# A decoder's cross attention and expert router read unnormalised rows; the norm's root is applied later

## The chip, the cores and the metric

One core of a Trainium2 chip runs the whole program. The metric is the device time of one execution in microseconds (us). The change is judged against the kernel before on the same chip.

## The reference, cut to what matters

Three layers run on 512 tokens of width 1024 in float32. The first two are hybrid layers (feed-forward, selective attention, RWKV-7, gated delta rule), which the change doesn't touch. The third mixes, attends to 256 memory rows, and sends each token to 2 of 16 experts:

```
h = h + hybrid_mixer(rms_norm_2(h, mix_norm[l]), ...)
h = h + memory_cross_attention(rms_norm_2(h, cross_norm[l]), mem_n, w_xq[l], w_xk[l], w_xv[l], w_xo[l])
h = h + hierarchical_moe(rms_norm_2(h, moe_norm[l]), w_router_group[l], ...)

rms_norm_2(x, gain): x * rsqrt(mean(x*x, -1) + EPS) * gain
memory_cross_attention: q = h @ w_xq (4 heads of 128);  s = q k^T * 128**-0.5;  softmax(s) v;  @ w_xo
hierarchical_moe:
    g_prob = softmax(h @ w_rg + b_rg)                 # 4 groups
    grp = argmax(g_prob); p_grp = g_prob[grp]
    e_logits = (h @ w_re + b_re)[group grp]           # 4 experts of that group
    top_p, top_i = top_k(softmax(e_logits), 2)
    gate = p_grp * top_p / sum(top_p)
    # rows of h are sorted by expert into blocks of 128 (23 blocks), each block goes through its expert,
    # and the results come back weighted by gate
```

The root `rsqrt(mean(x*x))` is one number per token. A product of an unnormalised row with a weight matrix can therefore be multiplied by it afterwards.

## The kernel before, in words

Each engine has its own program, written out by hand in order; engines meet through counted semaphores (`act.step(name)` raises one, `e.wait_ge(*act.at(name))` waits for it). The residual stream `xT` lies with channels on partitions, as 8 chunks of 128 x 512 tokens. Weights come through a ring of two 1 MB slots (`ring`), issued by SyncE in the order of `sources`; a slot's load waits until the slot's last holder has let go of it. After the ring's end SyncE streams the experts' weights in 1 MB pieces, six deep, four of them in `arena`.

Two kinds of product occur. **Split products**: ScalarE copies the weights to `w_hi` (rounded, `split_act`, L340), VectorE writes the remainder `w_lo` (`split_dve`, L344), the rows are split likewise into `x_hi` (L429 or L657) and `x_lo` (L434 or L661), and TensorE makes three passes of 128x512 for each product (hi*hi, lo*hi, hi*lo; L456, L469, L513, L652). **Whole products** take float32 operands as they are; TensorE shows two records for each.

A **norm** (`norm_pe`, `norm_act`, `norm_dve`): ScalarE squares the 8 chunks as the residual of each is done (L365), GpSimd adds seven of them (L372), TensorE sums over channels (`mean_pe`, L379), ScalarE takes the root (L384), VectorE the reciprocal (L389), TensorE spreads it over partitions (L394), and VectorE writes the normalised chunks `xn` (L420). In feed-forward layers the kernel before already works otherwise: `rows_act_in` makes `x_hi` (times the gain, without the root) and the square of each chunk right after its residual, `gate_first_pe` (L456) multiplies chunk by chunk, and the root is applied to the result.

Around the change the work stands in this order:

- `out_pe` of "mix2_out": four split slots, the last products at L513, each chunk's residual added by VectorE (L527).
- `cross_pe`, `cross_act`, `cross_dve`: the norm; queries for four heads by whole products (heads 0 and 1 chunk by chunk at L734, heads 2 and 3 at L718); ScalarE copies them out (L2716); both engines split the two slots of `w_xo` (XO_AT); then two strands of softmax attention (`attention_pe`, `attention_act`, `attention_dve`) run woven, 8 blocks each: scores (L1867), maximum (L1907), its negative times the scale (L1915), exponential (L1935), scaling (L1901), transposes (L1876), copy (L1946), values (L1885), copy (L1952).
- `out_pe` of "cross_out": two split slots (L652, L513), residuals.
- `router_pe`, `router_act`, `router_dve`: the norm; logits by whole products, 128x20 each (L734); 32 transposes that turn the rows to token order (L2748, copied out at L2770); VectorE splits the first three expert pieces (L2929), adds the bias (L2781), makes two softmaxes over groups and experts (`softmax4`, with exponentials on ScalarE at L2768 and L2773) with the choice of group and of two experts (up to `chosen`, L2840); TensorE ranks the tokens of each expert (L2752 to L2757); VectorE turns ranks into row numbers (`rows`, L2878).
- `experts_pool`: GpSimd scatters the token rows by eight indirect DMAs (L3080). SyncE loads the first two blocks of rows back, and the experts start (L2954, L3002, L3009, L2943).

Of the kernel before, what the change touches and what calls it, by code (L numbers as in the profile page):

```python
# [164 lines left out]
def build(nc, x_in, mem_in, const_in, w1_in, w2_in, y_out):  # L165
    with ExitStack() as ctx:
# [103 lines left out]
        for at, n, who in ((0, 17, pe), (17, 4, dve), (21, 2, pe), (23, 2, dve), (25, 1, pe)):  # L270
            slots(two_at + at, n, who)
# [280 lines left out]
        norm_order["cross"] = norm_order["moe"] = from_bank(0)  # L552

# [1298 lines left out]
        class Block:  # L1852
            def __init__(self, width, products, mask, values, part, dst):
                self.width, self.products, self.mask = width, products, mask
                self.values, self.part, self.dst = values, part, dst

# [33 lines left out]
        def attention_dve(e, M, blocks, first, scale):  # L1890
            tag, n = M.tag, len(blocks)
            for i in range(n + 2):
# [9 lines left out]
                if i < n:  # L1902
# [12 lines left out]
                    e.tensor_scalar(nm, mx, -scale, None, ALU.mult).then_inc(*dve.step(("nm", tag, g)))  # L1915
# [3 lines left out]
        def attention_act(e, M, blocks, first, scale):  # L1919
            tag, n = M.tag, len(blocks)  # L1920
            for i in range(n + 2):
# [5 lines left out]
                if i < n:  # L1927
# [4 lines left out]
                    if b.mask is None:  # L1932
                        if g >= 2:
                            e.wait_ge(*pe.at("turn", tag, g - 2))
                        e.activation(p_row, M.SCORES[:, :b.width], ACT.Exp, bias=nm, scale=scale, accum_out=sm).then_inc(  # L1935
                            *act.step(("exp", tag, g), ("read", tag, g)))
# [745 lines left out]
        def cross_room(F):  # L2682
            X, A = Room(), Arena(4 * SLOT)
            X.k_, X.v = F.k_mem, F.v_mem
            X.q_ = A.take(4 * SEQ).rearrange("p (c t) -> p c t", c=4)
            X.attend = [softmax_room(("cross", n), A, banks, at) for n, banks, at in (
# [3 lines left out]
        def cross_blocks(X, n):  # L2690
            blocks = []
            for q in range(NT):
                for h in (n, n + 2):
                    blocks.append(Block(
                        MEM, [(X.q_[:, h, q * P:(q + 1) * P], X.k_[:, h, :])], None,
                        lambda s, h=h: X.v[:, s, h * P:(h + 1) * P], slice(0, P), mixed[:, h, q * P:(q + 1) * P]))
            return blocks

        def cross_pe(e, X):
            norm_pe(e, "cross")  # L2700
            w = columns(XQ_AT)
            e.wait_ge(*there(XQ_AT))
            by_chunk(e, "cross", lambda c, n: (w[:, c, n * P:(n + 1) * P], xn[:, c, :]),
                     [bank[n][:, :] for n in range(2)]).then_inc(
                *pe.step(("cross_q", 0), ("cross_q", 1), ("slot", XQ_AT)))
            e.wait_ge(*there(XQ_AT + 1))
            for c in range(2):
                by_channel(e, XQ_AT + 1, c * P, bank[2 + c][:, :], xn).then_inc(
                    *pe.step(("cross_q", 2 + c), *([("slot", XQ_AT + 1)] if c else [])))
# [780 lines left out]
```

## Time and profile before

| what | before |
|---|---|
| median of 3 runs | 3636.42 us (3635.45 to 3636.93) |
| span of the profiled execution | 3662.9 us |
| TensorE busy | 3480.6 us, 95% |
| VectorE, ScalarE, GpSimd busy | 53%, 38%, 12% |
| mean granted TensorE clock | 0.949 of full |

The span is that of one execution under the profiler, from the first to the last instruction; it is the only time the profile gives of that execution, and it is 26.5 us (0.7%) above the median of the timed runs. In the rows below a time is us from the span's start; "busy" of TensorE counts matmuls whose ends are modelled; PEclk is the granted clock as a share of full speed, 1.00 or 0.50 for the two levels. What stands in brackets at a row's end is the idle time of that engine before it and what ended it.

### The profile page before, as it was taken

To read this page: it belongs to the slowest core of one execution; us is meant where nothing else is said; L and a number is where in the kernel's file an instruction comes from. 1 tells how busy PE (TensorE), PEld (TensorE's weight loads), DVE (VectorE), ACT (ScalarE), POOL (GpSimd) and SP (SyncE) were. 2 spreads that over 40 slices of the span, in tenths; PEclk is the share of its full clock that TensorE was granted. 3 is DMA by queue.
4 is the path that set the end of the run, shared out by engine and by line. 5 is a ranking of instruction groups with operands and counts; after the bars stand their busy time and mean duration, and the time that the engine had idled before them with its cause. 6 is when DMAs were issued, how large, how long until landed. Compare 5 with 4: busy or idle time off the path is not lost. (4 is left out here: it accounts for less than half of the span.)

```text
span 3662.9 us, 43142 instructions
## 1 busy us (share of the span) xinstructions
PE 3480.6 (95%) x17900; PEld 2807.1 (77%) x17900; DVE 1925.6 (53%) x2891; ACT 1383.2 (38%) x1924; POOL 431.8 (12%) x217
## 2 busy tenths in 40 slices
PE   8999998999999999999999999999999998699995
PEld 6888797876888888887878767888787675588884
DVE  4434457774453445343567754434344333489885
ACT  3222345533321232123455433222244333377772
POOL 1000342000100010002420001000131000122222
PEclk9999999986999999999989989999999999699997
DMA  4443220001223222222200002222220210599993
GB/s 173 148 144 109 81 81 1 1 24 47 81 92 111 92 93 92 104 92 81 92 13 1 1 24 107 100 94 92 109 88 27 78 58 35 224 372 408 408 408 142
DMA packets 65986, 414.61 MB, mean 113 GB/s; under 512 B 6912, under 2 KB 11136, under 8 KB 22272
## 3 DMA queue, kind: packets, MB, share of 16 engines
q1 hardware_dynamic: 63488, 403.46, 29.5%
q0 software_dynamic: 2304, 8.39, 0.6%
q8 instruction: 142, 2.33, 0.3%
q14 instruction: 52, 0.43, 0.0%
HBM read 375.13 MB, written 36.70 MB: 112 GB/s over the span
## 5 line engine op out<-in xcount | busy, mean ns | idle before, releaser
L344 DVE TENSOR_TENSOR w_lo<-ring,w_hi 128x2048 fp32r<-128x2048 f32 x146 | 334.5, 2291 | 869.6 <-ACT w_hi L340 869.6
L340 ACT ACTIVATE w_hi<-ring 128x2048 fp32r<-128x2048 f32 x146 | 280.3, 1920 | 1001.0 <-PE bank L469 584.5
L469 PE MATMUL bank<-x_hi,w_lo 128*128 128x512 f32 x1344 | 533.5, 397 | 0.0
L469 PE MATMUL bank<-x_hi,w_hi 128*128 128x512 f32 x1344 | 527.3, 392 | 0.0
L469 PE MATMUL bank<-x_lo,w_hi 128*128 128x512 f32 x1344 | 524.2, 390 | 0.0
L469 PEld LDWEIGHTS bank<-x_lo,w_hi 128*128 128x128 f32 x1344 | 252.3, 188 | 62.1
L469 PEld LDWEIGHTS bank<-x_hi,w_lo 128*128 128x128 f32 x1344 | 252.3, 188 | 58.0
L469 PEld LDWEIGHTS bank<-x_hi,w_hi 128*128 128x128 f32 x1344 | 252.3, 188 | 54.4
L513 PE MATMUL bank<-h_hi,w_hi 128*128 128x512 f32 x704 | 274.0, 389 | 0.0
L513 PE MATMUL bank<-h_hi,w_lo 128*128 128x512 f32 x704 | 274.0, 389 | 0.0
L513 PE MATMUL bank<-h_lo,w_hi 128*128 128x512 f32 x704 | 273.8, 389 | 0.0
L372 POOL TENSOR_TENSOR tmp<-tmp 128x512 f32<-128x512 f32 x54 | 76.1, 1409 | 1091.5 <-ACT tmp L365 1085.1
L2924 ACT ACTIVATE e_hi<-arena 128x2048 fp32r<-128x2048 f32 x92 | 176.3, 1916 | 23.9 <-PE bank L2943 21.1
L2929 DVE TENSOR_TENSOR e_lo<-ring,e_hi 128x2048 fp32r<-128x2048 f32 x45 | 150.1, 3335 | 44.3 <-ACT e_hi L2924 44.3
L2929 DVE TENSOR_TENSOR e_lo<-arena,e_hi 128x2048 fp32r<-128x2048 f32 x70 | 157.9, 2283 | 6.0 <-ACT e_hi L2924 6.0
L513 PEld LDWEIGHTS bank<-h_lo,w_hi 128*128 128x128 f32 x704 | 132.2, 188 | 27.6
L513 PEld LDWEIGHTS bank<-h_hi,w_lo 128*128 128x128 f32 x704 | 132.1, 188 | 27.5
L513 PEld LDWEIGHTS bank<-h_hi,w_hi 128*128 128x128 f32 x704 | 132.2, 188 | 27.4
L2934 POOL TENSOR_TENSOR e_lo<-arena,e_hi 128x2048 fp32r<-128x2048 f32 x22 | 102.0, 4634 | 318.3 <-ACT e_hi L2924 318.3
L703 PE MATMUL bank<-x_hi,ring_r 128*128 128x512 f32 x352 | 139.1, 395 | 0.0
L998 POOL TENSOR_TENSOR ring_r<-ring,first 128x1024 fp32r<-128x1024 f32 x6 | 14.4, 2421 | 1045.0 <-ACT first L990 1045.0
L998 POOL TENSOR_TENSOR ring_r<-ring,high 128x1024 fp32r<-128x1024 f32 x44 | 110.8, 2543 | 194.3 <-ACT high L990 194.3
(565 smaller groups left out, 6965.0 us busy)
## 6 DMA issues: line engine op xcount, KB each, us to landing
ring<-slots SPq DMA_DIRECT2D x238, 1024.0 KB, 4.8
arena<-slots SPq DMA_DIRECT2D x92, 1024.0 KB, 8.2
x_rows<-v_first SPq DMA_DIRECT2D x23, 512.0 KB, 6.8
xn<-x_rows SPq DMA_DIRECT2D x23, 512.0 KB, 7.9
y_rows<-xn SPq DMA_DIRECT2D x23, 512.0 KB, 8.5
x_aside<-xT SPq DMA_DIRECT2D x3, 2048.0 KB, 6.3
xT<-x_aside SPq DMA_DIRECT2D x3, 2048.0 KB, 7.9
xT<-x_t SPq DMA_DIRECT2D x2, 1024.0 KB, 10.4
```

Source lines behind the costliest of these rows:

```text
L340: e.activation(w_hi[:, k % 2, :], ring[:, k % RING, :], ACT.Copy).then_inc(*act.step(("hi", k)))
L344: e.tensor_tensor(w_lo[:, k % 2, :], ring[:, k % RING, :], w_hi[:, k % 2, :].bitcast(F32), ALU.subtract).then_inc(*dve.step(("slot", k)))
L372: e.tensor_tensor(SUM[:, :], SUM[:, :], squares[i][:, :], ALU.add).then_inc(*pool.step(("sum", tag, i)))
L469: made = e.matmul(bank[b + f][:, :], w.rearrange("p (k n) -> p k n", k=KC)[:, c, f * P:(f + 1) * P], (x_hi, x_lo)[part][:, c, :], start=c ...
L513: made = e.matmul(bank[d][:, :], w.rearrange("p (f n) -> p f n", f=2)[:, f, d * P:(d + 1) * P], rows[part][:, 2 * n + f, :], start=n == 0 ...
L703: made = e.matmul(out, w[:, c0:c0 + P], x, start=i == 0 and m == 0, stop=i == KC - 1 and m == 2)
L998: e.tensor_tensor(half_slot(ring_r[:, k % RING, :], half), raw, half_slot(high_of(N, n), half).bitcast(F32), ALU.subtract).then_inc(*pool. ...
L2924: e.activation(e_hi[m % W_BUFS][:, :], e_ring[m % E_RING], ACT.Copy).then_inc(*act.step(("expert_hi", m)))
L2929: e.tensor_tensor(e_lo[m % W_BUFS][:, :], e_ring[m % E_RING], e_hi[m % W_BUFS][:, :].bitcast(F32), ALU.subtract).then_inc(*dve.step(("expe ...
L2934: e.tensor_tensor(e_lo[m % W_BUFS][:, :], e_ring[m % E_RING], e_hi[m % W_BUFS][:, :].bitcast(F32), ALU.subtract).then_inc(*pool.step(("exp ...
```

## The change: what it does

- **Cross queries.** The rows are made as in the feed-forward layers: `rows_act_in` writes `x_hi` and squares, the residual loop of "mix2_out" writes `x_lo`, and `gate_first_pe` and `gate_up_pe` make the queries as split products of 2 x 48 passes. The two query slots (XQ_AT) are therefore split by ScalarE and VectorE. The root is applied per token inside the softmax: the exponential takes the column `X.plus` (root * 128**-0.5) as its scale, and the negated maximum is multiplied by `X.minus`. TensorE no longer spreads the root and VectorE no longer writes `xn`.
- **w_xo.** Slot XO_AT is split between the copies of queries 1 and 2. Slot XO_AT + 1 is split by a third strand of the weave, `later`, which lets eight turns of the attention pass first.
- **Router.** ScalarE writes `moe_rows` (chunk times gain, no root) into `xn` as the residuals come; the logits of all four token tiles go to one bank, chunk by chunk; the mean is taken before the last chunk. VectorE multiplies the 128x80 logits by the root and adds the bias in two instructions. The copies of the transposed rows take the root as their scale, and come before the splits of the expert pieces on ScalarE.
- **Choice and gates.** The choice is made on the logits; both softmaxes are gone from before `chosen`. Exponentials and gates are made once, after the row numbers: ScalarE's single exponential (128x20) stands after the expert splits, VectorE's three expert splits and five gate instructions after `slots`.

The diff, cut to its core:

```diff
@@ slots
-        for at, n, who in ((0, 17, pe), (17, 4, dve), (21, 2, pe), (23, 2, dve), (25, 1, pe)):
+        for at, n, who in ((0, 17, pe), (17, 4, dve), (21, 2, dve), (23, 2, dve), (25, 1, pe)):
...
@@ attention_dve, attention_act
-                    e.tensor_scalar(nm, mx, -scale, None, ALU.mult).then_inc(*dve.step(("nm", tag, g)))
+                    e.tensor_scalar(nm, mx, -scale if b.minus is None else b.minus, None, ALU.mult).then_inc(
+                        *dve.step(("nm", tag, g)))
...
+                        e.activation(p_row, M.SCORES[:, :b.width], ACT.Exp, bias=nm, scale=scale if b.scale is None else b.scale,
+                                     accum_out=sm).then_inc(*act.step(("exp", tag, g), ("read", tag, g)))
...
@@ cross
         def cross_pe(e, X):
-            norm_pe(e, "cross")
-            w = columns(XQ_AT)
-            e.wait_ge(*there(XQ_AT))
-            by_chunk(e, "cross", lambda c, n: (w[:, c, n * P:(n + 1) * P], xn[:, c, :]),
-                     [bank[n][:, :] for n in range(2)]).then_inc(
-                *pe.step(("cross_q", 0), ("cross_q", 1), ("slot", XQ_AT)))
...
+            gate_first_pe(e, "cross", XQ_AT, 0)
+            gate_up_pe(e, XQ_AT + 1, 2, None)
...
+        def later(split, e, k):
+            for _ in range(8):
+                yield
+            split(e, k)
+
         def cross_act(e, X):
-            norm_act(e, "cross", [dve.at("res", "mix2_out", 0, c) for c in range(KC)])
+            rows_act_in(e, "cross", par2("cross_norm"), [
+                [dve.at("res", "mix2_out", 0, c)] + ([pe.at("down", ("mix2_out", 0), 7)] if c >= 6 else [])
+                for c in range(KC)])
+            split_act(e, XQ_AT + 1)
+            root_act(e, "cross", side_of("cross"))
             for n in range(4):
-                e.wait_ge(*pe.at("cross_q", n))
+                e.wait_ge(*pe.at("used", XQ_AT + n // 2))
                 e.activation(X.q_[:, n, :], bank[n][:, :], ACT.Copy).then_inc(*act.step(("cross_q", n)))
-            for n in range(2):
-                split_act(e, XO_AT + n)
-            weave(*((1, attention_act(e, X.attend[n], cross_blocks(X, n), 0, P ** -0.5)) for n in range(2)))
+                if n == 1:
+                    split_act(e, XO_AT)
+            weave(*((1, attention_act(e, X.attend[n], cross_blocks(X, n), 0, P ** -0.5)) for n in range(2)),
+                  (1, later(split_act, e, XO_AT + 1)))
...
@@ router
         def router_pe(e):
...
+            for i, c in enumerate(norm_order["moe"]):
+                e.wait_ge(*act.at("moe_row", c))
+                if i == KC - 1:
+                    mean_pe(e, "moe", bank[7])
+                for t in range(NT):
+                    made = e.matmul(bank[0][:, 20 * t:20 * t + 20], moe_rows[c][:, t * P:(t + 1) * P], w[:, c, 0:20],
+                                    start=i == 0 and t == 0, stop=i == KC - 1 and t == NT - 1)
...
         def router_act(e):
...
+                e.activation(moe_rows[c], xT[:, c, :], ACT.Copy, scale=par2("moe_norm")[:, c:c + 1]).then_inc(
+                    *act.step(("moe_row", c)))
+                square_act(e, "moe", i, None)
+            root_act(e, "moe", bank[7])
...
         def router_dve(e):
-            norm_dve(e, "moe", par2("moe_norm"))
-            for n in range(LOOK):
-                split_expert_dve(e, n)
+            root_dve(e, "moe")
...
-            softmax4("groups", ex, logits[:, :, 0:4])
...
-            softmax4("experts", es, es)
...
+            for n in range(LOOK):
+                split_expert_dve(e, n)
+            second = col[:, 112:116]
+            e.wait_ge(*act.at("gates"))
+            e.tensor_reduce(mx, ex, AX, ALU.add).then_inc(*dve.step())
...
@@ scalar_program, vector_program
-            out_act(e, "mix2_out", OUT_AT[2], 4, None, {4: [dve.at("gla_out", NT - 1)]}, 2, 4)
+            out_act(e, "mix2_out", OUT_AT[2], 4, XQ_AT, {4: [dve.at("gla_out", NT - 1)]}, 2, 4)
```

The first place where the order matters is ScalarE from the queries into the attention. `w_hi` is a weight split, `tmp<-xT` a square, `arena<-bank 128x512` a copy of one head's queries, `arena,col<-bank,col` an exponential. Before:

```order
L340 ACTIVATE w_hi<-ring 128x2048 x2
L365 ACTIVATE tmp<-xT 128x512 x8
L384 ACTIVATE col<-bank,eps 128x4
L2716 ACTIVATE arena<-bank 128x512 x4
L340 ACTIVATE w_hi<-ring 128x2048 x2
L1935 ACT_TABLE_LOAD
L1935 ACTIVATE arena,col<-bank,col 128x256 x4
```

With the change, up to the split that stands inside the attention:

```order
L340 ACTIVATE w_hi<-ring 128x2048
L384 ACTIVATE col<-bank,eps 128x4
L2719 ACTIVATE arena<-bank 128x512 x2
L340 ACTIVATE w_hi<-ring 128x2048
L2719 ACTIVATE arena<-bank 128x512 x2
L1938 ACT_TABLE_LOAD
L1938 ACTIVATE arena,col<-bank,col 128x256 x4
L1949 ACTIVATE arena<-bank 128x256 x2
L1938 ACTIVATE arena,col<-bank,col 128x256 x2
L1949 ACTIVATE arena<-bank 128x256 x2
L1955 ACTIVATE mixed<-bank 128x128 x2
L340 ACTIVATE w_hi<-ring 128x2048
```

One of the two splits of `w_xo` has moved in front of the last two query copies, the other behind the third step of the attention; VectorE's `w_lo` of that slot stands between its third and fourth step likewise.

The second place is VectorE in the router, from the residuals to the choice of the group (`e_lo` is the remainder of an expert piece, `xn` a normalised chunk). Before:

```order
L527 SCALAR_TENSOR_TENSOR xT<-bank,xT 128x512 x8
L389 RECIPROCAL col<-col 128x4
L420 SCALAR_TENSOR_TENSOR xn<-xT,par,bank 128x512 x8
L2929 TENSOR_TENSOR e_lo_65<-arena,e_hi_61 128x2048
L2929 TENSOR_TENSOR e_lo_66<-arena,e_hi_62 128x2048
L2929 TENSOR_TENSOR e_lo_67<-arena,e_hi_63 128x2048
L2781 TENSOR_TENSOR col<-bank,par 128x20 x4
```

With the change, the same start, and the end behind the row numbers:

```order
L527 SCALAR_TENSOR_TENSOR xT<-bank,xT 128x512 x8
L389 RECIPROCAL col<-col 128x4
L2810 TENSOR_TENSOR col<-bank,col 128x80
L2813 TENSOR_TENSOR col<-col,par 128x80
L2834 TENSOR_REDUCE col<-col 128x4
...
L2902 CAST ids<-col 128x7
L2952 TENSOR_TENSOR e_lo_65<-arena,e_hi_61 128x2048
L2952 TENSOR_TENSOR e_lo_66<-arena,e_hi_62 128x2048
L2952 TENSOR_TENSOR e_lo_67<-arena,e_hi_63 128x2048
L2907 TENSOR_REDUCE col<-col 128x4
```

The eight normalised chunks are gone and the three splits stand behind the last cast of `ids`, where GpSimd scatters.

The third is TensorE in the router. Before:

```order
L513 MATMUL bank<-x_hi,w_lo 128x512
L379 MATMUL bank<-const,tmp 128x1 x8
L394 MATMUL bank<-const,col 128x128 x4
L734 MATMUL bank<-ring,xn 128x20 x32
L2748 MATMUL bank<-const,xn 128x128 x32
```

With the change:

```order
L513 MATMUL bank<-x_hi,w_lo 128x512
L2763 MATMUL bank<-ring,xn 128x20 x28
L379 MATMUL bank<-const,tmp 128x1 x8
L2763 MATMUL bank<-ring,xn 128x20 x4
L2772 MATMUL bank<-const,xn 128x128 x32
```

The logits stand directly behind the last output product, with the mean between the seventh and the eighth chunk.

## Rows read from the trace of the kernel before

**Rows 1.** Timeline of TensorE, end of mix2_out to the attention: start, us, instruction.

```profile
3024.04 0.39 PE L513 MATMUL bank<-x_hi,w_lo 128*128 128x512 f32 x1
3031.58 15.69 PE L734 MATMUL bank<-xn,ring 128*128 128x512 f32 x32 [0.93 <-DVE xn L420]
3047.11 13.90 PE L718 MATMUL bank<-xn,ring 128*128 128x512 f32 x32
3071.16 2.08 PE L1867 MATMUL bank<-arena 128*128 128x256 f32 x4 [8.33 <-ACT arena L1935]
3077.43 1.03 PE L1867 MATMUL bank<-arena 128*128 128x256 f32 x4
```

**Rows 2.** Timeline of ScalarE at the attention's start.

```profile
3061.05 0.60 ACT L2716 ACTIVATE arena<-bank 128x512 f32<-128x512 f32 x1 [6.27 <-PE bank L718]
3067.68 1.28 ACT L1935 ACT_TABLE_LOAD   x1
3070.54 0.47 ACT L1935 ACTIVATE arena<-bank,col 128x256 f32<-128x256 f32 x1 [1.58 <-DVE col L1915]
```

**Rows 3.** Timeline of TensorE in the router.

```profile
3119.59 0.39 PE L513 MATMUL bank<-x_hi,w_lo 128*128 128x512 f32 x1
3121.61 1.95 PE L379 MATMUL bank<-const,tmp 128*128 128x1 f32 x16 [1.64 <-POOL tmp L372]
3127.13 13.82 PE L734 MATMUL bank<-ring,xn 128*128 128x20 f32 x64 [0.93 <-DVE xn L420]
3140.78 5.39 PE L2748 MATMUL bank<-const,xn 128*128 128x128 f32 x32
```

**Rows 4.** Windows of the router: us, busy of PE, PEld, DVE, ACT, POOL, then PEclk, DMA, GB/s.

```profile
3120.00:3124.00 4.00, 1.95 (x16) 1.86 (x16) 0.80 (x2) 2.18 (x3) 1.42 (x2) 0.97 0.50 170
3136.00:3139.00 3.00, 3.00 (x16) 3.00 (x15) 2.20 (x1) 0.00 (x0) 0.00 (x0) 0.50 0.00 0
3153.00:3157.00 4.00, 3.60 (x16) 3.49 (x16) 0.77 (x7) 0.00 (x0) 0.00 (x0) 0.50 0.01 2
```

**Rows 5.** Timeline of VectorE in the router: ranks come back, row numbers are done.

```profile
3156.78 0.17 DVE L2850 TENSOR_SCALAR col<-bank 128x16 f32<-128x16 f32 x1 [3.13 <-PE bank L2757]
3159.87 0.17 DVE L2878 CAST ids<-col 128x8 int32<-128x8 f32 x1
```

**Rows 6.** GpSimd's first scatter, then TensorE's first turn of the experts' rows.

```profile
3160.90 1.17 POOL L3080 DMA_INDIRECT x_rows<-mixed,ids  x1 [39.34 <-issue]
3178.02 1.97 PE L2954 MATMUL bank<-const,xn 128*128 128x128 f32 x8 [21.28 <-DMA xn<-x_rows]
```

**Rows 7.** Layer 1's feed-forward start: TensorE, ScalarE, VectorE.

```profile
2257.57 0.39 PE L456 MATMUL bank<-x_hi,w_hi 128*128 128x512 f32 x1
2270.45 1.05 PE L394 MATMUL bank<-const,col 128*128 128x128 f32 x8
2252.76 0.71 ACT L429 ACTIVATE x_hi<-xT,par 128x512 fp32r<-128x512 f32 x1
2261.74 2.88 DVE L434 SCALAR_TENSOR_TENSOR x_lo<-xT,par,x_hi 128x512 fp32r<-128x512 f32 x2
```

**Rows 8.** Attention, third and fourth step: ScalarE, then VectorE.

```profile
3077.75 0.46 ACT L1952 ACTIVATE mixed<-bank 128x128 f32<-128x128 f32 x2
3078.71 0.47 ACT L1935 ACTIVATE arena<-bank,col 128x256 f32<-128x256 f32 x1 [0.50 <-DVE col L1915]
3076.64 0.15 DVE L1898 RECIPROCAL col<-col 128x1 f32<-128x1 f32 x1
3078.06 0.42 DVE L1907 TENSOR_REDUCE col<-bank 128x1 f32<-128x256 f32 x1 [0.88 <-PE bank L1867]
```

**Rows 9.** The page, splits on ScalarE and VectorE: busy, mean ns of one, idle before.

```profile
L340 ACT ACTIVATE w_hi<-ring 128x2048 fp32r<-128x2048 f32 x146 | 280.3, 1920 | 1001.0 <-PE bank L469 584.5
L2929 DVE TENSOR_TENSOR e_lo<-ring,e_hi 128x2048 fp32r<-128x2048 f32 x45 | 150.1, 3335 | 44.3 <-ACT e_hi L2924 44.3
L2929 DVE TENSOR_TENSOR e_lo<-arena,e_hi 128x2048 fp32r<-128x2048 f32 x70 | 157.9, 2283 | 6.0 <-ACT e_hi L2924 6.0
```

More of the change, by code:

```diff
@@ L2697, in cross_blocks @@
+                    blocks.append(b)
             return blocks
         def cross_pe(e, X):
-            norm_pe(e, "cross")
-            w = columns(XQ_AT)
-            e.wait_ge(*there(XQ_AT))
-            by_chunk(e, "cross", lambda c, n: (w[:, c, n * P:(n + 1) * P], xn[:, c, :]),
-                     [bank[n][:, :] for n in range(2)]).then_inc(
-                *pe.step(("cross_q", 0), ("cross_q", 1), ("slot", XQ_AT)))
[L2706 to L2709, printed above, removed]
+            gate_first_pe(e, "cross", XQ_AT, 0)
@@ L2721, in cross_dve @@
         def cross_dve(e, X):
-            norm_dve(e, "cross", par2("cross_norm"))
-            for n in range(2):
-                split_dve(e, XO_AT + n)
-            weave(*((1, attention_dve(e, X.attend[n], cross_blocks(X, n), 0, P ** -0.5)) for n in range(2)))
+            split_dve(e, XQ_AT + 1)
+            root_dve(e, "cross")
+            own(e, dve)
+            e.tensor_scalar(X.plus, rstd_col, P ** -0.5, None, ALU.mult).then_inc(*dve.step())
+            e.tensor_scalar(X.minus, rstd_col, -P ** -0.5, None, ALU.mult).then_inc(*dve.step())
@@ L2730, in build @@
+            split_dve(e, XO_AT)
+            weave(*((1, attention_dve(e, X.attend[n], cross_blocks(X, n), 0, P ** -0.5)) for n in range(2)),
+                  (1, later(split_dve, e, XO_AT + 1)))
         ids_row, ids_slot = ids[:, 0:8], ids[:, 8:15]
@@ new lines, in router_pe @@
+            made.then_inc(*pe.step(("logits",), ("slot", k)))
+            for t in range(NT):
+                for half in range(2):
+                    b, before = turned_bank(t, half), 2 * t + half - len(turned_banks)
+                    if before >= 0:
+                        e.wait_ge(*act.at("token_rows", before // 2, before % 2))
+                    for n in range(4):
+                        made = e.transpose(b[:, n * P:(n + 1) * P], moe_rows[4 * half + n][:, t * P:(t + 1) * P], ident)
+                    made.then_inc(*pe.step(("token_rows", t, half)))
@@ new lines, in router_act @@
+            root_act(e, "moe", bank[7])
+            for t in range(NT):
+                for half in range(2):
+                    e.wait_ge(*pe.at("token_rows", t, half))
+                    if t == 0 and half == 0:
+                        e.wait_ge(*dve.at("rstd", "moe"))
+                    e.activation(token_rows[:, t, 512 * half:512 * half + 512], turned_bank(t, half)[:, :], ACT.Copy,
+                                 scale=rstd_col[:, t:t + 1]).then_inc(*act.step(("token_rows", t, half)))
@@ L2779, in router_dve @@
             e.wait_ge(*pe.at("logits"))
[L2780 to L2783 removed]
+            own(e, dve)
+            e.tensor_tensor(logits, bank[0][:, 0:80].rearrange("p (t n) -> p t n", t=NT), wide(rstd_col, [P, NT, 20]),
+                            ALU.mult).then_inc(*dve.step())
```

103 lines of the change are left out of this document (43 added, 60 removed).

## The prediction

> **What bounds the kernel now.** I read the page first: TensorE is busy 95% of the span, so a change pays only where TensorE stands idle, runs at its lower clock, or does work that another form does faster. Then I took the timelines of TensorE, ScalarE and VectorE between the end of the mixer's output product and the first expert, about 157 us, because all that the change moves lies there; the instruction orders of the two kernels are the same up to the splits that feed this stretch.
>
> In the cross stage the last output product starts at 3024.04 and the next could start 0.23 us later, at 3024.27. The first query product starts at 3031.58, after the norm, and the queries take 15.69 and 13.90 us, until 3061.01 [rows 1]. The last copy of a query starts 0.04 us later, but the first exponential only at 3070.54: VectorE has to write both remainders of w_xo first, and the second slot is loaded late, since its ring slot is held until the queries are done [rows 2]. So 46.3 us pass between the output product and the first exponential.
>
> In the router the last product ends at 3119.82. The norm comes, then 64 records of 128x20 logits from 3127.13 to 3140.95, at 0.216 us each; the 32 transposes take 5.39 us [rows 3]. The granted clock is 0.97 over 3120 to 3124, then 0.50, and it stays there all through the logits. It is 0.50 again for the ranking products, whose 16 records are busy 3.60 us [rows 4]. VectorE receives the ranks at 3156.78 and has the row numbers at 3160.04 [rows 5]. The scatter starts 0.86 us later and TensorE turns the first rows at 3178.02 [rows 6]. From the row numbers on, nothing that TensorE waits for changes its length, so the expert stage and the end move as one block by what is gained ahead.
>
> **The change: cross stage.** Layer 1's feed-forward start is the same code and gives the measure. There 36 passes, the mean and 12 passes fill TensorE from 2257.57 to 2270.45, 12.9 us, without a gap [rows 7]. I copy that: 3024.27 + 12.9 = 3037.2. The second slot is 48 passes. The 36 passes before the mean there took 8.3 us, 0.231 each, so 11.1 us more: 3048.3, and its result is seen 0.16 us later. The added ScalarE work, x_hi (0.71, overlapping to about 0.62) and the square per chunk, fits into TensorE's 1.39 us per chunk. The added split of XQ_AT delays VectorE's residuals by about 2.3 us. In layer 1 it does so too, and the last x_lo ended at 2264.6, 7.1 us in, where TensorE wants it at 8.3 [rows 7]. This costs nothing, with 1.2 us to spare; were that gone, it would be paid one for one.
>
> After the queries: two copies, 1.1 us, then the table load of 1.28 us [rows 2], now on the path because VectorE has long split XO_AT. The scores and the maximum take 1.2 us beside it. First exponential: 3048.5 + 1.1 + 1.3 = 3050.9, against 3070.54. **Gain 19.6 us.**
>
> TensorE also arrives at full clock. Before, the first four score records of the first step took 2.08 us, and later ones 1.03 [rows 1]; some 0.5 us of that, in each of the first three steps, lay ahead of the maximum. **Gain 1.5 us.**
>
> Against it stands the third strand. Before, the third step's output copies end at 3078.21, and VectorE begins the fourth step at 3076.64 [rows 8]. Now ScalarE begins the split at 3078.21 on that clock and takes 1.9 us; VectorE waits for it and takes 2.28 us, as an arena split does [rows 9]. It begins the fourth step at 3082.35, 5.7 us late. Its pause of about 1 us between scaling and the next maximum then falls away, because the scores are ready [rows 8]. **Loss 4.7 us.** It could be 3 if the engines catch up more later, or 6.
>
> Every exponential now takes a column as scale too. x_hi, with one column, took 0.71 us on 512 elements, a plain copy of 512 took 0.60 [rows 2, 7]: 0.1 us each, 16 times, 1.6 us if all were on the path. I take 0. The loop is closed by VectorE and TensorE: each of VectorE's maxima waits for the scores, and these stand behind the values of the step before [rows 8]; the exponential has some 0.5 us of room. The Trainium skill speaks against the change here: "ScalarE: Activation LUTs", section "What ACT_TABLE_LOAD costs", says that each [128,1] pointer operand adds about 93 ns. The 0.11 us between the two rows agrees; by it 16 exponentials would cost 1.5 us if nothing hid them.
>
> Cross stage together: 19.6 + 1.5 - 4.7 = **16.4 us**. Output products, squares and residuals between the stages stay.
>
> **The change: router.** TensorE goes from the last product straight into the logits, as seven of eight chunks' rows are ready or come faster than they are used. I count from the last product, T0. The clock held for about 4 us after dense work ended [rows 4], so for 4 us I take full clock. No row has 128x20 records there. The nearest above is the mean's 0.122 us per record at full clock, below half of 0.216, 0.108 [rows 3]; I take 0.12, the row with the same weights. That is 33 of the 56 records; 23 more at 0.216 take 5.0. The mean, at half clock, is 3.7 (twice the 1.95 less some overlap), the last 8 records 1.7. Logits end at T0 + 14.4, where they ended at T0 + 21.1: **gain 6.7 us**. Ends of this: 9.6 if the clock never falls, 17.3 if it falls at once, so 11.5 or 3.8 gained.
>
> From the logits on, before: 19.1 us to the row numbers (3140.95 to 3160.04). Now: 23 VectorE instructions to the choice. The fifteen between the ranks' arrival and the row numbers took 3.26 us, 0.217 each [rows 5], so 5.0. TensorE's transposes take 5.4 (unless the clock is already full, then 3.5, and the choice decides). They were faster than 32 times 0.216, so the clock comes back during them [rows 3], and the ranks follow at once at full clock: half of 3.60, 1.9 with its wait. Then 3.3 us as before. Together 10.6: **gain 8.5 us**. The moved copies of token rows keep up: 0.7 against 0.85 us per four transposes at half clock; the ranks wait for the fourth only.
>
> **Under the scatter** VectorE now has three splits, 6.9 us, and five small ones, from 1.3 us after the row numbers; it is wanted 18 us after them [rows 6]. The time of the work itself is nothing. But both engines touch SBUF together. VectorE's split took 3335 ns in the form that mostly runs beside GpSimd's, against 2283 alone, 46% more [rows 9]. No row shows a scatter beside VectorE work. Nearest below is no effect; above, the eight issues of 0.95 to 1.17 us are held for the whole of the splits, 6.9 us. I take 1 us, between, nearer to nothing, since only five of the eight issues overlap and a stretch of 46% on these would be 2.2. The Trainium skill, "GPSIMD Engine Reference", section "Key points", says that GpSimd shares its SBUF interfaces with VectorE and contends with instructions that have two SBUF inputs, as these splits have. The slowed split agrees; for a scatter no row here shows it.
>
> Router together: 6.7 + 8.5 - 1.0 = **14.2 us**.
>
> **The sum.** 16.4 + 14.2 = 30.6 us. The profiled span would go from 3662.9 to about 3632. That execution is 26.5 us above the median of the timed runs, 0.7%. I see no reason why a stretch of 157 us should carry much of that, so I take the gain in full from the median: 3636.4 - 30.6 = **3606 us**, 0.8% faster. A measurement of this kernel can tell some 0.2%, 7 us, from no change.
>
> **The rivals.**
> - *The clock holds through the logits.* TensorE comes from dense work here, not from a pause as before. For it: nothing shows 128x20 records beginning at full clock. Against: it never rose in 13.8 us of them. Logits 4.8 us earlier; after them the choice decides: 5.0 + 1.9 + 3.3 = 10.2, 0.4 better. Time 3601. Chance 0.15.
> - *The woven split costs less.* The engines catch up in five further steps, or it costs 2 us. 3603. Against: the loop has little slack [rows 8]. Chance 0.10.
> - *The scatter is held by VectorE's splits*, 6.9 us in place of 1: 3612. Chance 0.12.
> - *The query stage breaks up.* x_lo comes later than in layer 1, TensorE pauses between chunks, and the clock falls for 4 us: 8 to 10 us lost, 3615. Against: the same code ran without a gap [rows 7]. Chance 0.08.
> - *The gain is not delivered*: some late load or wait keeps the attention's start where it was, and the router's logits wait for ScalarE's rows: within 7 us of before. Chance 0.02.
> - *Slower.* The experts' products begin after about 20 us of idle TensorE. If, after the changed stretch, the clock were not granted again there, each 1 MB piece of 12 passes, 0.231 us each, would take 5.6 us in place of 2.8. At 11 pieces of such clock the gain is gone, at 14 the time is 3645. Against: the attention's score records went from 2.08 to 1.03 us within 6 us of dense work [rows 1], and the experts' entry is as before. Chance 0.03.
>
> **How the numbers follow.** The forecast, 3606 give or take 3, has the remaining 0.50. The range takes in the clock and the cheap split, 3598 with both, and the held scatter and the broken query stage, up to 3617; outside are 0.05 for the last two cases and some 0.1 for combinations. Faster by over 0.2%: 0.95; within 0.2%: 0.02; slower: 0.03.
>
> **What would show it.** Right: the first exponential some 26.6 us after the last output product; a hole of 5 to 6 us on VectorE in the attention's fourth step; 128x20 records of 0.12 us that turn into 0.216 some 4 us in; the ranking records busy about 2 us; row numbers 25 us after the last cross product. Wrong: a gap between the passes of the first query slot, scatter issues longer than 1 us or gaps over 0.3 us between them, or another length than 485 us from the first turn of the experts' rows to the end.

## The result and the profile after

| | before | with the change |
|---|---|---|
| median of 20 timed runs, us | 3647.02 (3614.04 to 3666.89) | 3623.48 (3595.32 to 3652.71) |
| ratio of the two, 95% interval | 1 | 0.9931 (0.9909 to 0.9952) |
| span of the profiled execution, us | 3662.9 | 3600.6 |
| granted clock over that span | 0.949 | 0.963 |

The change is faster by 0.7%, some 25 us; 30.6 us would be a ratio of 0.9916, which lies in the interval. The time itself lies above the prediction's range of 3598 to 3617 us. Here and below, a ratio leaves out the runs counted as slow, over 1.5% above the fastest of the same kernel (here one of the change's, 3652.71), and so it is not the quotient of the medians. The three runs of before that were shown first, 3635.45 to 3636.93, are the first three of these 20: the other seventeen run from 3614.04 to 3666.89.

The two profiled spans differ by 62.3 us, and only part of that is the change. I cut each span at marks that both kernels have: the end of the last "mix2_out" product, the first exponential of the cross attention, its end (ScalarE's first `x_hi<-mixed`), the end of the last "cross_out" product, the row numbers (end of the cast to 128x8), TensorE's first turn of the experts' rows, the end. Lengths in us:

| stretch | before | after | difference |
|---|---|---|---|
| start to the end of mix2_out (code not touched) | 3024.3 | 2988.5 | -35.8 |
| to the first exponential | 46.27 | 26.76 | -19.5 |
| the attention | 24.98 | 31.69 | +6.7 |
| its output products | 24.30 | 25.91 | +1.6 |
| to the row numbers | 40.22 | 22.97 | -17.25 |
| to the first turn of the experts' rows | 17.98 | 20.31 | +2.3 |
| to the end | 484.88 | 484.44 | -0.4 |

From mix2_out to the end the sum is 638.63 before and 612.08 after: **26.55 us** gained. The other 35.8 us came ahead of anything that the change touches, and the experiments have to say what they are.

TensorE in the cross stage of after, timeline (start, us, instruction, idle before):

```profile
2988.52 0.39 PE L456 MATMUL bank<-x_hi,w_hi 128*128 128x512 f32 x1
3001.41 0.39 PE L469 MATMUL bank<-x_hi,w_hi 128*128 128x512 f32 x1
3013.83 1.13 PE L1869 MATMUL bank<-arena 128*128 128x256 f32 x4 [1.17 <-ACT arena L2723]
3015.99 1.80 PE L1869 MATMUL bank<-arena 128*128 128x256 f32 x4 [1.02 <-ACT arena L1938]
3022.01 1.03 PE L1869 MATMUL bank<-arena 128*128 128x256 f32 x4
3027.58 0.69 PE L1878 MATMUL bank<-const,arena 128*128 128x128 f32 x2 [4.54 <-DVE arena L1903]
3030.81 1.91 PE L1869 MATMUL bank<-arena 128*128 128x256 f32 x4
```

It answers to [rows 1]. The first query slot begins 0.23 us after the last output product and lasts 12.89 us without a gap. The scores come 12.42 us later. Then 4.54 us of idle TensorE behind VectorE in the fourth step, and the scores after it take 1.91 us where a step earlier they took 1.03.

ScalarE there, which answers to [rows 2, 8], and VectorE:

```profile
3013.80 1.28 ACT L1938 ACT_TABLE_LOAD   x1
3015.28 0.56 ACT L1938 ACTIVATE arena<-bank,col 128x256 f32<-128x256 f32 x1 [0.20 <-DVE col L1917]
3022.80 1.94 ACT L340 ACTIVATE w_hi<-ring 128x2048 fp32r<-128x2048 f32 x1
3028.14 0.56 ACT L1938 ACTIVATE arena<-bank,col 128x256 f32<-128x256 f32 x1 [3.40 <-DVE col L1917]
```

```profile
3024.77 2.29 DVE L344 TENSOR_TENSOR w_lo<-ring,w_hi 128x2048 fp32r<-128x2048 f32 x1 [3.40 <-ACT w_hi L340]
3026.98 0.15 DVE L1900 RECIPROCAL col<-col 128x1 f32<-128x1 f32 x1
3031.90 0.42 DVE L1909 TENSOR_REDUCE col<-bank 128x1 f32<-128x256 f32 x1 [2.30 <-PE bank L1869]
3038.04 0.42 DVE L1909 TENSOR_REDUCE col<-bank 128x1 f32<-128x256 f32 x1 [0.82 <-PE bank L1869]
3041.03 0.42 DVE L1909 TENSOR_REDUCE col<-bank 128x1 f32<-128x256 f32 x1 [0.82 <-PE bank L1869]
```

The hole is 3.40 us of waiting and 2.29 us of split. Undisturbed steps follow each other every 2.99 us.

TensorE in the router, which answers to [rows 3]:

```profile
3072.88 7.45 PE L2763 MATMUL bank<-ring,xn 128*128 128x20 f32 x56
3080.17 3.55 PE L379 MATMUL bank<-const,tmp 128*128 128x1 f32 x16
3083.58 1.87 PE L2763 MATMUL bank<-ring,xn 128*128 128x20 f32 x8
3085.29 5.04 PE L2772 MATMUL bank<-const,xn 128*128 128x128 f32 x32
```

Its windows (us, busy of PE, PEclk, DMA share, GB/s), which answer to [rows 4]:

```profile
3073.00:3077.00 4.00, 4.00 (x39) 1.00 0.53 166
3077.00:3078.00 1.00, 1.00 (x10) 0.91 0.97 410
3084.00:3085.00 1.00, 1.00 (x6) 0.50 1.00 426
3088.00:3089.00 1.00, 1.00 (x11) 0.97 1.00 410
```

The granted clock is full (2.4 GHz) from the first 128x20 record, at 3072.88, to about 3077.8, 4.9 us, as the 0.91 of the second window tells. In that time 45 records begin, one every 0.11 us; from there on it is half (1.2 GHz) and one begins every 0.21 us. It stays there for the mean and the last chunk, and is back during the transposes. VectorE and GpSimd at the scatter, which answer to [rows 5, 6]:

```profile
3095.68 0.17 DVE L2889 CAST ids<-col 128x8 int32<-128x8 f32 x1
3097.03 6.68 DVE L2952 TENSOR_TENSOR e_lo<-arena,e_hi 128x2048 fp32r<-128x2048 f32 x3
```

```profile
3096.71 1.17 POOL L3103 DMA_INDIRECT x_rows<-mixed,ids  x1 [20.98 <-issue]
3098.19 1.95 POOL L3103 DMA_INDIRECT x_rows<-mixed,ids  x1 [0.30 <-issue]
3100.45 1.89 POOL L3103 DMA_INDIRECT x_rows<-mixed,ids  x1 [0.30 <-issue]
3102.64 1.90 POOL L3103 DMA_INDIRECT x_rows<-mixed,ids  x1 [0.30 <-issue]
3104.84 0.95 POOL L3103 DMA_INDIRECT x_rows<-mixed,ids  x1 [0.30 <-issue]
```

The three issues that lie under the splits take 1.9 us each, the next one 0.95 again. (An issue is the time that GpSimd spends on starting one indirect DMA.)

### The profile page after: what moved, and what is told of

It reads as the page before. It is cut to its first block, busy times and chain, and to the rows that moved or that the text cites. A ratio compares the mean times of both kernels' runs of the same rounds, so it can differ in the third digit from the quotient of the medians.

```text
span 3600.6 us, 43178 instructions
## 1 busy us (share of the span) xinstructions
PE 3434.2 (95%) x17916; PEld 2781.4 (77%) x17916; DVE 1924.2 (53%) x2877; ACT 1397.4 (39%) x1941; POOL 436.4 (12%) x217
## 4 chain that ended last, share of the span: by engine, by line
PE 90%; DVE 5%; ACT 2%; POOL 1%; DMA 1%; issue 1%; DVEq 0%; SPq 0%; POOLq 0%; ACTq 0%
PE bank L469 26%; PE bank L513 15%; PE bank L2966 11%; PE bank L704 7%; PE bank L710 5%; PE bank L1869 3%; PE bank L851 2%; PE bank L860 2%; PE bank L1887 2%; PE bank L456 2%; PE bank L653 1%; PE bank L1878 1%; PE bank L869 1%; DMA ring<-slots 1%; POOL tmp L372 1%
```

## The experiments

Each is named by what stands in it. "Stretch" is mix2_out to the end in the profiled execution, 638.63 before and 612.08 with the change.

**One half each.** x1 has the router of before (`router_pe`, `router_act` and `router_dve` put back) and the new cross stage. x2 has the cross stage of before and the new router:

```
-        for at, n, who in (..., (21, 2, dve), ...):
+        for at, n, who in (..., (21, 2, pe), ...):
-            out_act(e, "mix2_out", OUT_AT[2], 4, XQ_AT, ...)
+            out_act(e, "mix2_out", OUT_AT[2], 4, None, ...)
```

with `cross_room`, `cross_blocks`, `cross_pe`, `cross_act` and `cross_dve` put back.

> The cross stage of the change with the router of before. Stage X runs from the end of mix2_out's last product to the end of cross_out's last product: 95.6 us before, 84.4 with the change; stage R from there to the row numbers: 40.2 and 23.0; stage S from the row numbers to TensorE's first turn of the experts' rows: 18.0 and 20.3. Theory 1, the two halves don't touch: X 84.4, R 40.2, S 18.0, so 11.2 us less than before. Theory 2, the cross stage's gain needs the other half or is partly a free gift of the clock: X off by over 2 us. The stretch ahead of stage X, which no edit touches, differed by 35.8 us between the two profiles; by theory 1 it goes on wandering by tens of us with the granted clock, and the ratio of times is 0.997 give or take that.

> The router of the change with the cross stage of before. Theory 1 (halves independent): X 95.6, R 23.0, S 20.3, so 17.2 - 2.3 = 14.9 us less than before, ratio 0.996. Theory 2: R or S off by over 2 us.

x1: stretch 625.28, 13.35 us gained, ratio 0.9992 (0.9962 to 1.0023). x2: 624.81, 13.8 us gained, ratio 0.9986 (0.9952 to 1.0021). The two halves make 27.2 us together, the whole change 26.55: they add up within 0.6 us, and neither needs the other. In x1 the stages outside the cross stage have their lengths of before (40.64 and 17.93 us), in x2 the cross stage has (95.69). Two stages are off what was expected by more than the repeats differ: x1's cross stage is 82.8 us and not 84.4, because its output products keep their length of before, and x2's way to the row numbers is 24.1 and not 23.0; both are taken up below. The ratios put either half at less, with intervals that just hold the stage lengths; what the timed runs add, below, says how.

**The split of slot XO_AT + 1 taken out of the attention**, and made where the cross output's own first work is done:

```
-            weave(*((1, attention_act(...)) for n in range(2)),
-                  (1, later(split_act, e, XO_AT + 1)))
+            weave(*((1, attention_act(...)) for n in range(2)))
...
-            out_act(e, "cross_out", XO_AT, 2, None, {...}, 2)
+            out_act(e, "cross_out", XO_AT, 2, None, {...}, 1)
```

and the same on VectorE.

> The change, but slot XO_AT + 1 is split behind the rows of the cross output instead of inside the attention. The forecast priced the woven split at 4.7 us. Theory A, it cost more because TensorE's idle stretch of 4.5 us let its clock fall (the next steps and the start of cross_out's products ran at 0.50): X falls from 84.4 to about 75 to 77, and no 0.50 stands in the attention after its start. Theory B, the price was the hole alone: X 79 to 80. Theory C, the split has to be paid wherever it stands: X 84. The late split has 11 us of first-slot products as cover.

x3: stretch 604.73, 7.3 us shorter than the change and 33.9 shorter than before; ratio 0.9959 (0.9927 to 0.9991). The 33.9 us would be a ratio of 0.9907, which this interval doesn't hold: the timed runs show only 3 to 27 us of it. That is taken up below. The attention takes 24.49 us instead of 31.69 and the output products 24.33 instead of 25.91; the way from the last product to the row numbers takes 24.09 instead of 22.97, though its code is the same. ScalarE, VectorE and TensorE at the moved split:

```profile
3053.93 1.90 ACT L340 ACTIVATE w_hi<-ring 128x2048 fp32r<-128x2048 f32 x1
```

```profile
3055.86 2.29 DVE L344 TENSOR_TENSOR w_lo<-ring,w_hi 128x2048 fp32r<-128x2048 f32 x1 [0.87 <-ACT w_hi L340]
```

```profile
3065.07 0.39 PE L513 MATMUL bank<-x_hi,w_hi 128*128 128x512 f32 x1
```

The slot is ready at 3058.15 and wanted at 3065.07, so there it costs nothing: 6.9 us to spare, and no gap before the product. In the attention's fourth step nothing was to spare. In this execution the granted clock also stayed at 1.00 through the attention, where that of the change fell:

```profile
3024.00:3028.00 4.00, 1.84 (x8) 1.00 0.00 0
3028.00:3032.00 4.00, 3.19 (x14) 1.00 0.00 0
```

**And VectorE's splits kept off the scatter.** x4 is x3 with two more edits: GpSimd marks the end of its eight issues, and VectorE waits for the mark before the three expert splits.

```
+            e.memset(col2[:, 110:111], 0.0).then_inc(*pool.step(("issued",)))
...
+            e.wait_ge(*pool.at("issued"))
             for n in range(LOOK):
                 split_expert_dve(e, n)
```

> x3, and VectorE's three expert splits wait until GpSimd has issued all eight scatters. Theory A, the three issues of 1.9 us (in place of 0.95) are slowed by VectorE's splits beside them: all eight issues 0.95 to 1.17, S falls from 20.3 to 18.0 or a little above, since the splits still end ahead of the first rows (row numbers + 10.9 + 6.7 + 1 = 18.6, wanted at 19.9). Theory B, the slow issues come from the expert weights' transfers of that time: the issues stay at 1.9, S 20.3. Together with x3 some 36 to 38 us less than before.

x4: ratio 0.9939 (0.9903 to 0.9975), stretch 604.82. GpSimd, VectorE and TensorE there:

```profile
3129.43 1.18 POOL L3102 DMA_INDIRECT x_rows<-mixed,ids  x1 [22.12 <-issue]
...
3138.47 0.95 POOL L3102 DMA_INDIRECT x_rows<-mixed,ids  x1 [0.30 <-issue]
```

```profile
3139.58 6.70 DVE L2951 TENSOR_TENSOR e_lo<-arena,e_hi 128x2048 fp32r<-128x2048 f32 x3 [9.74 <-POOL col L3104]
```

```profile
3146.53 1.97 PE L2976 MATMUL bank<-const,xn 128*128 128x128 f32 x8 [21.27 <-DMA xn<-x_rows]
```

Every issue is back at 0.95 us, and the row numbers to the first turn take 17.97 us, as before the change: the 2.3 us were the splits' doing. The splits end 0.25 us before TensorE begins, which still waits for the DMA alone, so the wait costs nothing. The stretch as a whole did not fall under that of x3, since the cross stage took 2.3 us more, and so the 36 to 38 us expected for both edits together came to 33.8. Its granted clock in the attention's second step is that of the change again:

```profile
3053.40:3055.40 2.00, 1.35 (x4) 0.78 0.00 0
3055.40:3057.40 2.00, 2.00 (x8) 0.50 0.00 0
```

Up to this point x3 and x4 are the same program. Both idle for 1.2 us before the first scores and 1.0 after; one lost the clock there, the other did not. So some 2 us of a stage depend on how the execution falls, not on the code. x9, the same kernel as x4, has 77.9 us in the cross stage as x4 has, against 75.6 in x3.

**Both kernels once more, unedited.** x5 is before, x6 is the change.

> The kernel before, unedited, against itself. Theory 1 (the stretch ahead of stage X wanders with the granted clock, whatever the kernel): its time in stage X and after is 638.6 us within 2, its stretch ahead of it anywhere from 2987 to 3030, single times spread over 40 us or more, and the ratio is off 1 by up to 0.003. Theory 2 (the changed kernels run ahead of stage X differently than the kernel before): the stretch ahead is 3024 again and times agree within 0.3%.

> The change, unedited, beside x5 on this chip. Theory 1: 612.1 us within 2 from stage X on, and a ratio of 0.993 within 0.003. Theory 2: the part ahead of stage X is longer than in x5 by some 10 us on the average of the runs, ratio 0.996.

x5: 0.9991 (0.9954 to 1.0029), which is how well this set tells nothing from nothing: 0.4% either way. x6: 0.9942 (0.9914 to 0.9970). The stretch of x5 is 638.39 (638.63), of x6 611.64 (612.08): repeatable to 0.5 us. But x5's span is 3621.7, and that of the first profile of the same kernel 3662.9. The whole 41 us lie ahead of the changed stretch. The largest piece is the first layer's mixer: from the end of the feed-forward ahead of it to the end of its own last product it takes 574.2 us in one and 545.0 in the other. Windows in it, before, then x5:

```profile
820.00:840.00 20.00, 19.78 (x83) 0.50 0.00 1
840.00:860.00 20.00, 20.00 (x75) 0.50 0.00 0
```

```profile
820.00:840.00 20.00, 19.91 (x136) 1.00 0.01 2
840.00:860.00 20.00, 20.00 (x143) 0.93 0.01 1
```

The same instructions with TensorE busy in both, granted 0.50 in one execution and 1.00 in the other. In the profile of after both windows have 1.00, and the mixer takes 549.5 us. That is where 24.7 of its extra 35.8 us came from, and since two executions of the kernel before differ as much, I call it luck and not the change's doing.

**The columns in the softmax.** Both stand on x3. x7 gives the exponential a number as its scale again; x8 gives one to the negated maximum as well. Both leave the norm's root out of the softmax (the two columns hold the constant alone), so their results are not those of the kernel; the instructions keep their shapes and order, and each was run once:

```
-   e.activation(p_row, ..., ACT.Exp, bias=nm, scale=scale if b.scale is None else b.scale,
+   e.activation(p_row, ..., ACT.Exp, bias=nm, scale=scale,
...
-   e.tensor_scalar(nm, mx, -scale if b.minus is None else b.minus, None, ALU.mult)
+   e.tensor_scalar(nm, mx, -scale, None, ALU.mult)
```

> x3 with the exponential's scale as an immediate again (the root is left out of the softmax, the columns hold the constant): only the negated maximum still reads a column. x3's attention steps take 2.99 us in the steady part, before's 2.93. Theory A (the exponentials' pointer is hidden, the 0.06 is VectorE's small instruction with a column, 0.21 in place of 0.15 us): steps stay 2.99, the exponential goes from 0.56 to 0.47. Theory B (the exponentials are on the path, 0.09 each): steps 2.90 or less.

> x7 with the negated maximum's factor as an immediate too (the root is left out of the softmax altogether). Theory A: steps 2.93. Theory B: as x7.

x7, ScalarE, VectorE, and TensorE at the second step:

```profile
3030.10 0.47 ACT L1938 ACTIVATE arena<-bank,col 128x256 f32<-128x256 f32 x1 [0.50 <-DVE col L1917]
```

```profile
3026.86 0.21 DVE L1917 TENSOR_SCALAR col<-col 128x1 f32<-128x1 f32 x1
3029.39 0.42 DVE L1909 TENSOR_REDUCE col<-bank 128x1 f32<-128x256 f32 x1 [0.81 <-PE bank L1869]
3032.38 0.42 DVE L1909 TENSOR_REDUCE col<-bank 128x1 f32<-128x256 f32 x1 [0.82 <-PE bank L1869]
```

```profile
3019.86 1.80 PE L1869 MATMUL bank<-arena 128*128 128x256 f32 x4 [0.93 <-ACT arena L1938]
```

x8, VectorE:

```profile
3060.48 0.43 DVE L1909 TENSOR_REDUCE col<-bank 128x1 f32<-128x256 f32 x1 [0.88 <-PE bank L1869]
3060.94 0.15 DVE L1917 TENSOR_SCALAR col<-col 128x1 f32<-128x1 f32 x1
3063.41 0.43 DVE L1909 TENSOR_REDUCE col<-bank 128x1 f32<-128x256 f32 x1 [0.88 <-PE bank L1869]
```

In x7 the exponential is back from 0.56 to 0.47 us and the undisturbed step stays at 2.99: there its column costs nothing. In x8 VectorE's multiplication goes from 0.21 to 0.15 and the step to 2.93, that of before (3081.00 to 3083.93 there, at full clock). At the two ends of the attention it is otherwise, for there TensorE waits for ScalarE: ahead of the second step's scores it idles 0.93 us in x7 and 1.02 in the kernels with the column. The whole attention takes 24.98 us in x7 against 25.23 in x4 and x9, which have the same half clock in its first steps, so the exponential's column costs 0.25 us. With the clock full throughout it takes 23.80 in x8 against 24.49 in x3, so both columns cost 0.7 us, and some 0.4 of it is VectorE's.

**The best version again.** x9 is x4, in a set of its own.

> x4 once more, unedited. From stage X on it should take 603 to 605 us, 34 us less than before, and 7 less than the change; S 18.0 again. If the gain reaches the time, the ratio is 0.991 within 0.003, and at equal granted clock it lies below the change by some 6 to 7 us. Rival: part of what x3 and x4 gain in the stages is lost ahead of them, and the ratio stays at 0.994 or more, as x4's first timing had it.

x9: 0.9909 (0.9873 to 0.9945), median 3611.79 beside 3648.80 for before. Its stretch is 604.78 us. It beats before; against the change as it is, x4 and x9 are 7 us shorter in the stretch, which the medians of different sets can't tell.

**What the timed runs add.** Every timed run comes with its span and mean granted clock. Twice the missing clock times the span is about the time spent at half clock: 252 us for the fastest of the change's 20 runs (3595.32 us, clock 0.965), 372 us for the slowest (3652.71, 0.949). Within these 20 runs time and clock correlate at -0.99. One line with a common slope, fitted through the 98 timed runs of the change, x1 to x6 and x9 and the 69 runs of before beside which the experiments were timed (for the 20 of before in the first table no clock is on record), has 0.41 us of time per us at half clock and misses a run by 2.3 us. Beside before, at the same time at half clock, it puts the change at -17.8 us, x6 at -17.5, x1 at -11.1, x2 at -8.3, x3 at -21.3, x4 at -24.5, x9 at -23.5 and x5 at +0.1 (give or take 1 to 2). To this belongs the half-clock time that the edit itself removes, read from windows over the stretch up to the experts: 64.5 us before, 45.2 with the change, 62.3, 50.9, 33.4, 40.9 and 40.9 in x1, x2, x3, x4 and x9. With 0.41 for each of these:

| | fit | removed half clock x 0.41 | together | stretch shorter by |
|---|---|---|---|---|
| change | 17.8 | 7.9 | 25.7 | 26.55 |
| x1 | 11.1 | 0.9 | 12.0 | 13.35 |
| x2 | 8.3 | 5.6 | 13.9 | 13.8 |
| x3 | 21.3 | 12.8 | 34.1 | 33.9 |
| x4 | 24.5 | 9.7 | 34.2 | 33.8 |
| x9 | 23.5 | 9.7 | 33.2 | 33.85 |

Two ways that share only the granted clock agree within 1.4 us in every row. It is a fit, and the clock is given to three digits, so I take it as support for the stage lengths and not as a finer measurement.

The fit compares at the same time at half clock, and so it can't tell whether the edits change that time ahead of the stretch. x1 to x4 were timed together, against the same 35 runs of before, and all four gained less by the ratio than by the stretch, by 9 to 12 us in x1, x2 and x4 and by 19 in x3. Their runs spent 322, 316, 314 and 317 us at half clock on average and those of before 311 (standard errors 10 to 14 and 7), although their own stretches hold 2 to 31 us less of it: 13 to 34 us more ahead of the stretch, in code that no edit touches. In the two other sets, each on another chip, nothing of the kind stands: x6 has 24 us less at half clock than before, of which its stretch explains 19, and x9 23 less, of which its stretch explains 24; x9's ratio is 0.9909 where its stretch alone gives 0.9907. Whether the four were chance or something that the edits do to the clock ahead of them isn't settled.

## Why the prediction was right and wrong

Most mechanisms came as predicted, and together they gave 26.55 us where 30.6 was said; the time did not, because of the number that the gain was taken off. Of the 17.5 us between 3606 and 3623.5 the base is 10.6 and the mechanisms 4.1; the other 3 are within the ratio's interval. With the base right the same gain gives 3616.4, inside the range; with the gain right and the base wrong it is 3609.9.

**The base: wrong, and this put the time above the range.** "I see no reason why a stretch of 157 us should carry much of that, so I take the gain in full from the median": true of the gain, and of no use for the time. I took three runs within 1.5 us as this kernel's time and the profiled 3662.9, 26.5 us above them, as an oddity. It was the one sign on the page that the kernel wanders, and it stood in no bound. Over 20 runs the median is 3647.0, 10.6 above the three. The range was all mechanisms, with nothing in it for runs that lie 53 us apart.

**The query stage: right.** 26.76 us from output product to first exponential (26.6 predicted), no gap in the first slot, 19.5 us gained against 19.6. The copy from layer 1 held, x_lo's spare time included.

**"TensorE also arrives at full clock. Gain 1.5 us": wrong.** It arrives so, idles 1.17 and 1.02 us at the first two steps, and the clock falls in the second; the next two groups of scores take 1.80 and 1.70 us, hardly less than the 2.08 before. Only x3 and x8 kept the clock. x3's attention was then 0.5 us shorter than before's with the columns in it, and x8's 1.2 without them, so the 1.5 were nearly right for a clock that is kept. The row with 2.08 us stood behind 8.33 us of idle time, so I charged the loss to the long wait that would go. The short ones that stay came with the same fall in x1, x4, x6, x7 and x9 as well, and without it in x3 and x8. What decides between the two stays open.

**The woven split, "Loss 4.7 us": mechanism right, size too small.** It is 31.69 us against 25.23 in x4 (which has the same clock at the start): 6.5. VectorE began the fourth step 11.7 us after the first exponential, in x4 5.9: 5.8 late, where I had 5.7. I then gave back 1.0 because "the scores are ready". They were, once. But TensorE had idled 4.54 us, and its records in the fourth and fifth step ran at half clock:

```profile
3026.00:3027.00 1.00, 0.00 (x0) 0.81 0.00 0
3028.00:3032.00 4.00, 3.65 (x15) 0.50 0.00 0
3032.00:3034.00 2.00, 2.00 (x11) 0.64 0.00 0
```

VectorE waited 2.30 us for scores in the fifth step instead of 0.82. The pause was gained and lost again. In the change, x1 and x6, all with the split in this place, TensorE's half clock behind the stall lasts 6.8 us; in x3, x4 and x9, without it, there is none in the fourth and fifth step. So here the stall cost its own time and that of the records after it.

**The columns: a term taken at nothing that was 0.7 us.** I took 0 for the exponential's: 0.09 us dearer each, hidden in the undisturbed steps, 0.25 us at the ends. The Trainium skill, "ScalarE: Activation LUTs", section "What ACT_TABLE_LOAD costs", has 93 ns for it; the trace agrees with that price (0.47 to 0.56 us), but of the 1.5 us that I estimated from it for sixteen only the 0.25 appear. The other column, in VectorE's multiplication, I didn't cost: 0.06 us a step, 0.4 us in all.

**The output products, "stay": 1.6 us longer**, by half clock at their start (0.50 over 3051 to 3052). In x1 they took 24.33 with the split woven in, in x4 25.90 without it, so the woven split isn't the cause. Both executions of the change have it, and both of x4's kernel; what sets it stays open. The 1.1 us by which the router's way to the row numbers differs between the change and x3 are the clock's too: in the runs that take 24.1 us (x2, x3, x4, x9) half clock lasts 13.7 us in the logits, the mean and the transposes, in those that take 23.0 (the change, x6, x7, x8) 10.2. What ends it sooner stays open as well. The cross stage gained 11.2 where I had 16.4: 3.5 of the 5.2 missing in the attention, 1.6 here, 0.1 in the query stage.

**The logits: right in kind, too dear in size.** The clock held and fell, as taken, but after 4.9 us (3.9 in x2 and x3, 4.6 in x4 and x9) where I had 4, and a record took 0.11 us where I had 0.12. So the 56 records took 7.45 us where I had 33 at 0.12 and 23 at 0.216, 9.0; the mean 3.55 (3.7). They end 12.57 us after the last product (14.4). The rival of a clock that holds throughout falls. Logits to row numbers: 10.4 against 10.6.

**Under the scatter, "I take 1 us": too small, in the bounds.** 2.3 us. I had 2.2 for a stretch of 46% over five issues; it is 100% over three, and x4 shows the cause. Issues over 1 us were my own sign of being wrong, and they came. I also misread the row behind the 46%: its mean of 3335 ns covers two kinds of split. About half of them take 2.28 us, as alone. The others, which begin under GpSimd's own split, take 4.45, 95% more, as here in before, GpSimd and then VectorE:

```profile
3208.38 4.63 POOL L2934 TENSOR_TENSOR e_lo<-arena,e_hi 128x2048 fp32r<-128x2048 f32 x1 [37.52 <-ACT e_hi L2924]
3210.71 4.46 DVE L2929 TENSOR_TENSOR e_lo<-ring,e_hi 128x2048 fp32r<-128x2048 f32 x1 [3.14 <-ACT e_hi L2924]
```

So the trace of before already had the doubling. The Trainium skill, "GPSIMD Engine Reference", section "Key points", speaks of contention with instructions of two SBUF inputs, and here the trace shows it for the issue of an indirect DMA.

**The router together** gained 14.9 (14.2), and the experts ran 484.4 us (485): the slower rival has nothing for it. Over the stretch: 11.2 + 14.9 + 0.4 for the end is 26.55, where 30.6 was said. The mechanisms were 4 us too kind: 5.2 in the cross stage, most of it a clock that was taken for kept, against 0.7 gained in the router.

## What to carry to other kernels

Where executions of one kernel differ by more than a change is worth, compare the lengths of the touched stages between marks that both kernels have, and forecast the ratio; the absolute time needs a spread of its own, and three close runs don't give it. A split belongs where its consumer is far off and no loop waits for the engine, not inside a loop of short dependent steps: the same 4.2 us of work cost 6.5 us in the fourth step of the attention and nothing 11 us ahead of its product. And if TensorE is stalled in a stretch of short products, price the stall and the half clock that can follow it. A mean over instructions of one form can hide two kinds: look at single ones before taking it as the price of an overlap.

## What the runs showed of the hardware

- The same dense products got a granted clock of 0.50 over 40 us in one execution and 0.93 to 1.00 in another, of the same kernel, with TensorE busy in both. What decides that isn't known; nothing here tried to set it.
- One us at half clock cost 0.41 us of the kernel's time over 167 runs, not 0.5. Some of it costs nothing: in the change the clock is at half for the 20 us from the row numbers to the first turn, where TensorE does nothing.
- Issues of indirect DMAs on GpSimd took 0.95 us alone and 1.89 to 1.95 beside a VectorE `TENSOR_TENSOR` of 128x2048 with two inputs in SBUF. Such an instruction on VectorE took 2.28 us alone and 4.45 when it began under the same one on GpSimd.
- A column in place of a number cost a VectorE `TENSOR_SCALAR` of 128x1 0.06 us (0.15 to 0.21), a ScalarE exponential of 128x256 0.09 (0.47 to 0.56).
- Records of 128x20 begun at full clock came every 0.11 us for 3.9 to 4.9 us and only then every 0.21, close to the 0.216 that before's trace has throughout.
- Waits of 1.2 and 1.0 us between short products were followed by half clock in six profiled executions and not in two others (x3, x8), with the same waits to 0.15 us.
